# Attention's values stationary on half the array's columns, two heads side by side, and every second copy of the probabilities on VectorE

## The reference

```python
s = jnp.einsum('bhrnqd,bhrnkd->bhrnqk', qb, kb, ...) * scale
s = jnp.where(mask, s, jnp.finfo(jnp.float32).min)
m = jnp.max(s, axis=-1, keepdims=True)
p = jnp.exp(s - m)
denom = jnp.sum(p, axis=-1, keepdims=True)
o = jnp.einsum('bhrnqk,bhrnkd->bhrnqd', p, vb.astype(jnp.float32)) / denom
```

```python
outs.append(o); lses.append(lse)        # for (128,1), (512,4), (2048,16)
...
wts = jax.nn.softmax(jnp.stack(lses, axis=0), axis=0)
o = jnp.sum(wts[..., None] * jnp.stack(outs, axis=0), axis=0)
```

## Time and profile before

| | |
|---|---|
| median of 3 runs | 2057.57 us (2053.98 to 2057.8) |
| the profiled execution | 2056.82 us, span 2054.8 us |
| mean granted clock of PE, of full speed | 0.991 |
| PE busy | 1998.7 us (97%) |
| DVE, ACT, POOL busy | 1328.2, 844.9, 941.9 us |
| attention stage, first score matmul to first `q_out` | 1147.41 to 1304.64 us |

### The profile page before, as it was taken

One profiled execution on the slowest core, in us unless ns is written; L12 is line 12 of the kernel. 1 busy time (PEld: TensorE's weight loads), 2 busy tenths in 40 slices (PEclk: granted clock), 3 DMA queues, 4 the chain that ended last, 5 costly groups with the idle time before them and its releaser, 6 DMA issues.

```text
span 2054.8 us, 27393 instructions
## 1 busy us (share of the span) xinstructions
PE 1998.7 (97%) x10021; PEld 1658.6 (81%) x10021; DVE 1328.2 (65%) x1753; ACT 844.9 (41%) x1344; POOL 941.9 (46%) x548
## 2 busy tenths in 40 slices
PE   7999999999999999999999899998999999999997
PEld 6888888888887778878888689876888888888886
DVE  7887777756537654786231544698865565566977
ACT  5444454345411024562200676657333323334453
POOL 1354464333333468843453200665755555444553
PEclk8999999999999999999999999999999999999998
DMA  9223212211112243132110200132333233257344
GB/s 282 73 83 113 79 64 102 92 31 31 52 52 57 67 173 125 62 138 99 51 51 0 83 1 1 61 104 73 118 122 107 86 113 107 92 182 248 102 136 162
DMA packets 179500, 193.97 MB, mean 94 GB/s; under 512 B 9863, under 2 KB 122968, under 8 KB 179418
## 3 DMA queue, kind: packets, MB, share of 16 engines
q1 hardware_dynamic: 172996, 178.53, 27.3%
q10 hardware_dynamic: 6422, 14.37, 1.9%
HBM read 151.71 MB, written 41.16 MB: 94 GB/s over the span
## 4 chain that ended last, share of the span: by engine, by line
PE 81%; DVE 10%; ACT 4%; issue 3%; POOL 1%; DMA 0%; DVEq 0%; SPq 0%; ACTq 0%; POOLq 0%
PE psum L999 7%; PE psum L1538 7%; PE psum L1539 6%; PE psum L1540 6%; PE psum L1001 6%; PE psum L1000 6%; PE psum L1160 3%; PE psum L1641 3%; PE psum L1643 3%; PE psum L1642 3%; PE psum L1441 3%; PE psum L1020 3%; PE psum L1021 3%; PE psum L1019 3%; PE psum L1430 2%
## 5 line engine op out<-in xcount | busy, mean ns | idle before, releaser
L792 POOL TENSOR_TENSOR w_hi<-w_raw,ones 128x1024 fp32r<-128x1024 f32 x60 | 149.3, 2489 | 480.3 <-PE psum L1001 356.1
L999 PE MATMUL psum<-h_hi,w_hi 128*128 128x512 f32 x704 | 284.2, 404 | 0.0
L1001 PE MATMUL psum<-h_hi,w_lo 128*128 128x512 f32 x704 | 274.7, 390 | 0.0
L1000 PE MATMUL psum<-h_lo,w_hi 128*128 128x512 f32 x704 | 274.2, 389 | 0.0
L1673 ACT ACTIVATE arena<-psum 128x1024 f32<-128x1024 f32 (+7 forms) x134 | 100.1, 753 | 220.5 <-PE psum L1001 136.1
L795 POOL TENSOR_TENSOR w_lo<-w_raw,w_hi 128x1024 fp32r<-128x1024 f32 x60 | 168.0, 2800 | 4.7
L1000 PEld LDWEIGHTS psum<-h_lo,w_hi 128*128 128x128 f32 x704 | 132.4, 188 | 28.3 <-issue 2.6
L999 PEld LDWEIGHTS psum<-h_hi,w_hi 128*128 128x128 f32 x704 | 132.3, 188 | 28.4 <-issue 2.6
L1001 PEld LDWEIGHTS psum<-h_hi,w_lo 128*128 128x128 f32 x704 | 132.1, 188 | 28.5
L1641 PE MATMUL psum<-w_hi,h_hi 128*128 128x512 f32 x308 | 121.2, 394 | 3.1 <-DVE h_lo L3257 3.1
L989 POOL TENSOR_TENSOR w_lo<-arena,w_hi 128x512 fp32r<-128x512 f32 x61 | 86.1, 1415 | 75.7 <-ACT w_hi L1673 75.7
(11 more groups left out here) (485 smaller groups left out, 5289.0 us busy)
## 6 DMA issues: line engine op xcount, KB each, us to landing
w_raw<-w_in SPq DMA_DIRECT2D x64, 512.0 KB, 3.8
act_op<-arena SPq DMA_DIRECT2D x77, 256.0 KB, 2.3
arena<-act_op SPq DMA_DIRECT2D x77, 256.0 KB, 2.7
w_raw<-w_gate SPq DMA_DIRECT2D x22, 512.0 KB, 4.0
w_raw<-w_up SPq DMA_DIRECT2D x22, 512.0 KB, 5.2
arena<-ada_w SPq DMA_DIRECT2D x16, 512.0 KB, 7.2
arena<-w_out SPq DMA_DIRECT2D x16, 512.0 KB, 5.9
out_T<-arena SPq DMA_DIRECT2D x16, 512.0 KB, 5.6
```

The lines of the kernel that those rows point to most:

```text
L999: pe.matmul(o, wh, xh, start=(k == 0), stop=False)
L1000: pe.matmul(o, wh, xl, start=False, stop=False)
L1001: return pe.matmul(o, wl, xh, start=False, stop=(k == KT - 1))
```

## The change

1. `pv(m)` now does a pair of heads. The values (128 keys by 64 channels) are stationary, on the lower half of the array's columns for the even head and on the upper half for the odd one, and the transposed probabilities are moving, 128 columns. The result is channels by queries: even head on PSUM partitions 0 to 63, odd head on 64 to 127.
2. Since it is transposed, it must be turned back: for every four heads VectorE copies 128x256 to SBUF (`o_move`), PE transposes two 128x128 blocks (`back`), and VectorE divides from there in one instruction of 256 columns in place of two of 128 (`attended`).
3. `pt_copy` of odd steps is on VectorE, of even steps on ScalarE, with three buffers `probs_t` in place of two.
4. PE's round becomes `qk_pair(m)`, `p_t(2m-2)`, in even rounds `back`, `pv(m-2)`, `p_t(2m-1)`. The squares of `att_o` rows come three steps later on ScalarE, and at the end VectorE does `o_move(15)` ahead of the first `q_lo`.

```diff
-        probs_t = [page(22 + i) for i in range(2)]
+        probs_t = [page(i) for i in (22, 20, 23)]
+        o_t = page(26)[:, 128:384]
...
-            def pv(n):
-                i, h = n // AH, n % AH
-                pe.wait_ge(pt_done, n + 1)
-                if n >= AH:
-                    pe.wait_ge(ao_done, (n - AH) // 4 + 1)
+            def pv(m):
+                i, p = m // (AH // 2), m % (AH // 2)
+                pe.wait_ge(pt_done, 2 * m + 2)
+                if p % 2 == 0 and m >= 4:
+                    pe.wait_ge(ao_done, m // 2 - 1)
                 for j in range(i + 1):
-                    mm = pe.matmul(two_banks(3)[:, h * P:(h + 1) * P], blocks128(probs_t[n % 2], j),
-                                   v_b[:, j, (h // 2) * P:(h // 2 + 1) * P], start=(j == 0), stop=(j == i))
+                    for e in range(2):
+                        mm = pe.matmul(psum[DH * e:DH * e + DH, 6 + p // 2, (p % 2) * P:(p % 2 + 1) * P],
+                                       v_b[:, j, (2 * p + e) * DH:(2 * p + e + 1) * DH],
+                                       blocks128(probs_t[(2 * m + e) % 3], j), start=(j == 0), stop=(j == i))
                 mm.then_inc(pv_full, 1)
+            def back(g):
+                pe.wait_ge(ot_moved, OT_MOVED + g + 1)
+                for q in range(2):
+                    mm = pe.transpose(psum[:, 6 + g % 2, (2 + q) * P:(3 + q) * P], blocks128(o_t, q), ident[:])
+                mm.then_inc(ot_full, 1)
...
+            def o_move(g):
+                dve.wait_ge(pv_full, 2 * g + 2)
+                if g:
+                    dve.wait_ge(ot_full, OT_FULL + g)
+                dve.tensor_copy(o_t, psum[:, 6 + g % 2, 0:2 * P]).then_inc(ot_moved, 1)
...
+            def pt_copy(n):
+                w = (n // AH + 1) * P
+                dve.wait_ge(pt_full, n + 1)
+                if n >= 3:
+                    dve.wait_ge(pv_full, (n - 3) // 2 + 1)
+                dve.tensor_copy(probs_t[n % 3][:, 0:w], two_banks(2)[:, 0:w]).then_inc(pt_done, 1)
...
-                if n >= 6 and n % 4 == 2:
-                    attended((n - 6) // 4)
+                if n >= 7 and n % 4 == 3:
+                    o_move((n - 7) // 4)
+                if n >= 9 and n % 4 == 1:
+                    attended((n - 9) // 4)
+                if n >= 3 and n % 2:
+                    pt_copy(n - 2)
...
             q_raw_copy(5)
+            attended(2 * NT - 2)
             q_raw_copy(7)
+            o_move(2 * NT - 1)
             q_lo(0, "P1", 0)
+            q_lo(1, "P1", 1)
             attended(2 * NT - 1)
-            for j in range(1, 3):
-                q_lo(j, "P1", j)
+            q_lo(2, "P1", 2)
```

More of the change, by code:

```diff
@@ L190 @@
 N_SGU, N_SGU_SQ, N_SGU_NORM = 8, 17, 28
+OT_MOVED, OT_FULL = 5, 2
 T_ORDER = [4, 5, 6, 7, 0, 1, 2, 3]
@@ L474, in program @@
             sem("pv_full"), sem("den_done"), sem("ao_done"))
+        ot_moved, ot_full = lb_step, silu_done
         out_sent, mixn_done = sem("out_sent"), sem("mixn_done")
@@ L895, in q_sum @@
                 elif name == "S3":
+                    pool.wait_ge(pv_full, AH * NT // 2 - 1)
                     pool.wait_ge(*raw_ready(4 + j))
@@ L1459, in _ @@
             N = AH * NT
-            for m in range(N // 2 + 2):
+            for m in range(N // 2 + 1):
                 if m < N // 2:
                     qk_pair(m)
[L1463 to L1479, removed]
+                else:
+                    pe.wait_ge(mixn_done, NT)
+                    pe.wait_ge(s_moved, N)
+                    q_transpose(4)
+                    q_transpose(5)
+                if 0 <= 2 * m - N_SGU < SGU_G:
+                    sgu(2 * m - N_SGU)
+                if m >= 1:
+                    p_t(2 * m - 2)
+                if m >= 4 and m % 2 == 0:
+                    back(m // 2 - 2)
+                if m >= 2:
+                    pv(m - 2)
+                if 0 <= 2 * m + 1 - N_SGU < SGU_G:
+                    sgu(2 * m + 1 - N_SGU)
+                if m == N // 2:
+                    pe.wait_ge(*raw_ready(4))
+                    q_transpose(6)
+                    pe.wait_ge(*raw_ready(5))
+                    q_transpose(7)
+                if m >= 1:
+                    p_t(2 * m - 1)
+            pv(N // 2 - 1)
             def q_out(n, j, t):
@@ L1519, in _ @@
                     mm.then_inc(o_step, 1)
+                if n == 0:
+                    back(2 * NT - 1)
             for t in range(4):
@@ L2060, in pt_copy @@
                 act.wait_ge(pt_full, n + 1)
-                if n >= 2:
-                    act.wait_ge(pv_full, n - 1)
-                copy(probs_t[n % 2][:, 0:w], two_banks(2)[:, 0:w]).then_inc(pt_done, 1)
+                if n >= 3:
+                    act.wait_ge(pv_full, (n - 3) // 2 + 1)
+                copy(probs_t[n % 3][:, 0:w], two_banks(2)[:, 0:w]).then_inc(pt_done, 1)
             def mix_square(x, i, t, col_):
@@ L2098, in _ @@
             for n in range(N + 2):
-                if n >= 2:
+                if n >= 2 and (n % 2 == 0 or n == N + 1):
                     pt_copy(n - 2)
@@ L2115, in _ @@
                     root(M_SGU)
-                if n >= N_SGU_NORM and n % 8 == 4 and (n - 12) // 8 < NT - 1:
-                    for t in range(0 if n == N_SGU_NORM else (n - 12) // 8, (n - 12) // 8 + 1):
+                if n >= N_SGU_NORM and n % 8 == 7 and (n - 15) // 8 < NT - 1:
+                    for t in range(0 if n == N_SGU_NORM + 3 else (n - 15) // 8, (n - 15) // 8 + 1):
                         act.wait_ge(ao_done, 2 * t + 2)
@@ L2984, in _ @@
             dve.wait_ge(bias_in, 16)
+            def o_move(g):
[3 more added lines that the diff above has]
+                dve.tensor_copy(o_t, psum[:, 6 + g % 2, 0:2 * P]).then_inc(ot_moved, 1)
             def attended(m):
                 i, hh = m // 2, m % 2
-                dve.wait_ge(pv_full, 4 * m + 4)
                 dve.reciprocal(r_den[:, 4 * hh:4 * hh + 4], den_[:, 4 * m:4 * m + 4]).then_inc(den_done, 1)
                 dve.wait_ge(den_done, m + 1)
[L2992 to L2998, removed]
+                dve.wait_ge(ot_full, OT_FULL + m + 1)
+                o = att_o[:, i, hh * 256:(hh + 1) * 256].rearrange("p (h d) -> p h d", d=DH)
+                src = psum[:, 6 + hh, 2 * P:].rearrange("p (h d) -> p h d", d=DH)
+                r = r_den[:, 4 * hh:4 * hh + 4].rearrange("p (h x) -> p h x", x=1).to_broadcast([P, 4, DH])
+                TT(o, src, r, ALU.mult).then_inc(ao_done, 1)
             def q_raw_copy(k):
```

1 line of the change is left out of this document (added).

## The result

The changed kernel takes 2030.51 us (median of 4 runs, 2029.22 to 2032.28) beside 2057.22 us (4 runs, 2053.98 to 2057.8) of the kernel before, measured together: ratio 0.9876 [0.9865, 0.9888], 26.7 us less. The forecast had the sign and the mechanism, but 15.7 us less, and a range that ended at 2036.

What follows compares the result with a forecast made beforehand. PE was taken to bound five to seven blocks, ScalarE three and four. 9.3 + 4.3 + 1.5 + 3.8 - 3.2 = 15.7 us less gave 2041.1 us profiled, 2041.9 as median; range 2036 to 2055.

Steps and rivals of the forecast that it cites:

- three and four blocks: Attention rounds at three and four key blocks: ScalarE bounds them and loses eight copies, 4.3 us less.
- the cost of a block: Products of a head pair per key block in `pv`: 0.25 us in place of 0.446, bounds 0.223 and 0.27.
- the end: Behind the last `q_transpose`: first output step 2.3 us later, 0.9 us more up to step 4, together 3.2 us more.
- five to seven: Attention rounds at five to seven key blocks, bound by PE: 14.1 less 4.8, so 9.3 us less.
- eight: Eight key blocks up to the last `q_transpose`: 15.4 us of products become 11.6, 3.8 us less.
- Rival 1: Column halves do not run side by side in `pv`: 0.446 us a block, sum +13.1, 2070.7 us; chance 0.13.
- rival 2: Loads in `pv` stand in line, two of four not hidden: 0.358 us a block, about 2057 us; chance 0.13.
- The mode changes: PE entering and leaving half-column mode around each group of products: together 0.29 us.
- Rival 3: On PE's rounds, mode changes cost double (0.6 us) or VectorE's copies come late: 2046 to 2050 us; chance 0.18.
- One and two blocks: Attention rounds at one and two key blocks: three rounds by 0.5, 1.5 us less, bounds 0 and 3.
- VectorE's copies are covered: Odd steps' copies at eight blocks: 1.284 us and 0.15 for signals beside 1.60 us of scores, 0.17 to spare.
- The chain to step 4: Output steps 0 to 4: `attended(15)` waits for `back(15)`, delaying squares, root and rest, 0.9 us more.

Runs made afterwards that it cites:

- back_inside: Changed kernel with the two full transposes of `back` moved into the middle of the products of `pv`, one mode change more there and back: 2036.67 us, ratio 0.9911.
- squares_early: Changed kernel with ScalarE's squares of attention's rows back where they were (n % 8 == 4): 2036.33 us, ratio 0.9903.
- squares_late: Kernel before with only ScalarE's squares of attention's rows moved three steps later: 2054.64 us, ratio 0.9994.
- copies_split: Kernel before with only the odd steps' copies of transposed probabilities moved to VectorE, still two buffers: 2053.22 us, ratio 0.9989.
- both_on_before: Kernel before with both the later squares and the odd copies on VectorE, products on the full array: 2054.13 us, ratio 0.9989.
- in_turn: Changed kernel with the two loops of `pv` exchanged, all products of the even head ahead of the odd head's: 2048.68 us, ratio 0.9966.
- copies_act: Changed kernel with all copies of the transposed probabilities on ScalarE again: 2041.43 us, ratio 0.9922.
- rest_first: Changed kernel with VectorE's first `q_lo` put ahead of `o_move(15)`: 2031.2 us, ratio 0.9883.
- same_half: Changed kernel with both heads' products on the lower half of the columns, without accumulation over key blocks: 2060.18 us, ratio 1.0023.

## Why the prediction was wrong in its size

The mechanism was right and the sum too small. The step that failed is the one on three and four blocks; the cost of a block and the end were sized wrongly as well. By its own steps:

- **The cost of a block.** Taken 0.25 us, bounds 0.223 and 0.27; measured 0.22, the lower bound. Over 72 blocks at five to seven that is 2.2 us more, over 38 at eight 1.1 more: 9.3 becomes 11.5 for a measured 11.24, 3.8 becomes 4.9 for 5.01. Four loads of 64 columns a block hide entirely. Rival 1 (0.446) and rival 2 (0.358) are out. The Trainium skill, "TensorE: Matmul & The Clock Gate", section "The mechanism", has a sentence by which loads overlap only with matmuls of another row group, which would have given rival 2, though the same section also lets a load into the background weight buffer go ahead of running matmuls. Here both halves use all 128 rows, and two instructions, each with a load of its own, start every 0.109 us. (The 0.243 us of a full matmul in the prediction holds a pause of 0.57 us at 1312.69; the starts stand 0.227 us apart, and the argument stays as it was.)
- **The mode changes.** 0.29 a pair taken; `back_inside` gave 0.25 and 0.31. Right. Rival 3's double price is out.
- **Three and four blocks: the step that failed.** The prediction said that ScalarE "loses four copies of 0.484 and four of 0.596 us", 4.3 us, and stopped there. It overlooked that the diff takes the three squares, 3 x 0.81 = 2.4 us of ScalarE, out of this stretch too, and that PE's 27.26 us held 1.2 us of a lowered clock. ScalarE came to 21.50 in place of 24.1 us busy and PE to 22.31 in place of 25.0: 28 blocks at 0.22 and 8 rounds at 0.38 make 3.3 less, from 26.1 at full clock 22.8. PE is then the bound, and the stretch took 23.25, not 26.5. `squares_early` shows 1.87 of the 3.3 us as the squares', with the clock at 1.00 in both kernels. The 1.2 of the clock are read from PE's busy time in `squares_late`, `copies_split` and `both_on_before`; together they make 3.1 of 3.3.
- **One and two blocks.** 1.5 forecast, 1.34 measured, with bounds 0 and 3. No experiment took this apart, and executions of kernels that are the same up to there differ by up to 0.8 us in it (25.41 and 26.25 for before and `squares_late`).
- **VectorE's copies are covered.** No wait of PE for L3041 is among the waits; the copy of 1024 columns takes 1.23 us beside 1.58 us of scores. Right.
- **The end.** `pv(31)` started at T + 2.15 (forecast 2.1), PE waited 1.11 us for ScalarE ahead of it (forecast 1). Its products were through at T + 4.1, not 4.6, by the cheaper blocks. The first rest took 0.84 us (1278.97 to 1279.80), not 1.43, so step 0 came at T + 5.60, not 6.7; as the last section shows, a rest's length goes with an instruction of POOL beside it. The chain to step 4, put at 0.9 without a working, cost nothing: `attended(15)` was through 2.8 us later against step 0, but behind it stands one rest, of 0.71 us (1283.74), where before there were two, of together 3.47 us (L3010 at 1305.54). They end 4.4 us behind step 0 in both kernels. The diff moves the second `q_lo` ahead of `attended(15)`, which the prediction did not reckon with. The place and the order of the waits up to step 0 were right, the size 1.9 us too large.

In sum the forecast missed 8.2 us of the stage: 3.3 at three and four blocks, 3.2 by the cost of a block, 1.9 at the end, less 0.2 at one and two. The three large ones went the same way, and the range, which let only the block's price, the early rounds and the end vary, did not reach there. No one of them alone bridges the 5.5 us between the range's end at 2036 and the measured 2030.51. The medians missed by 11.0 us; the 2.8 beyond the 8.2 are not explained, and are of the size by which single executions differ.

## What to carry to other kernels

Where an operand is only half the array wide, two independent products on the two halves of the columns cost one, if they alternate in the program. That is shown here for fp32, 128 rows, 64 columns a half and 128 moving columns. A pair of such products saved 0.22 us, so a group is worth its change of mode (0.27 us there and back) from two pairs on. When an edit speeds the bound of one stretch, list every instruction that the diff moves out of the neighbouring engine's stretch, the small ones at its edge too, and ask of each busy time at which granted clock it was read. An edit that is worth 0.15% by itself was worth 0.5% beside one that sped up another engine, so undo edits on the changed kernel as well as adding them to the old one.

## What the runs showed of the hardware that I had not expected

**PE works ahead into the other half.** With the heads in turn, `in_turn`, some six starts around the border of the heads stand 0.05 us apart and not 0.109. How far this goes with a longer queue, or on what it depends, was not tried.

**Standing can be paid twice.** `copies_act` shows it most plainly. PE stands 2.07 us up to 1284.12, and the products behind take 3.63 us for the 1.97 of the changed kernel. Windows around that place, PEclk as the share of the full clock:

```profile
1282.00:1284.00 2.00, 0.06 (x1) 0.00 (x0) 0.57 (x1) 2.00 (x4) 2.00 (x2) 1.00 0.47 125
1284.00:1286.00 2.00, 1.88 (x18) 1.88 (x20) 0.00 (x0) 2.00 (x5) 2.00 (x3) 0.55 0.38 141
1286.00:1287.00 1.00, 1.00 (x14) 1.00 (x12) 0.00 (x0) 1.00 (x3) 1.00 (x2) 0.50 0.00 0
```

The granted clock is at 0.50 there, the lower of its two levels (1.2 for 2.4 GHz). Four kernels have the same instructions from the last `q_transpose` to step 4 and differ in how long PE stands there ahead of step 0 (stretch less PE's busy time): 1.35 us in all in `rest_first`, 2.60 in the changed kernel, 3.21 in `squares_early`, 3.51 in `back_inside`. The first two were granted 1.00 in the output steps and took 13.26 and 13.24 us; the last two 0.88, and took 14.44 and 14.42. In `back_inside` the last wait is 2.40 us, up to 1284.56; then:

```profile
1284.00:1285.00 1.00, 0.44 (x2) 0.43 (x3) 1.00 (x2) 0.29 (x1) 1.00 (x1) 1.00 0.00 0
1286.00:1287.00 1.00, 1.00 (x4) 0.81 (x3) 0.08 (x1) 0.00 (x0) 1.00 (x1) 0.50 0.00 0
```

Standing as the cause fits these five kernels, but no run changed it alone, and its length is not the whole of it: `same_half` stood 3.23 us in that place (7.97 less 4.74 busy), the last wait 2.12, with 3.71 us of products between its two waits for 1.97, and was granted 1.00 in the output steps, which took 11.49 us.

The longer standing itself comes from the two rests on VectorE, 2.54 us in the changed kernel, 3.14 in `squares_early` and 3.44 in `back_inside` for the same instructions. So 2.1 us of `back_inside` and 1.8 of `squares_early` lie outside of the place where the edit was made.

**How long a rest takes follows POOL.** The traces show what goes with a longer rest. The first rest of the changed kernel, alone, and POOL's instruction beside it; then the same two of `back_inside`:

```profile
1277.97 1.28 POOL L914 TENSOR_TENSOR arena<-spare 128x512 f32<-128x512 f32 x1
1282.48 1.28 POOL L914 TENSOR_TENSOR arena<-spare 128x512 f32<-128x512 f32 x1
1282.55 1.75 DVE L3034 TENSOR_TENSOR q_first<-spare,q_first 128x512 fp32r<-128x512 f32 x1
```

In the changed kernel the rest starts at 1278.97, POOL's instruction ends at 1279.25 and the rest at 1279.80, 0.55 us behind it. In `back_inside` the rest starts only 0.07 us behind POOL's instruction, which ends at 1283.76, and ends at 1284.30, again 0.55 behind. It is so in 49 of the 52 rests into `q_first` of the thirteen traces (0.54 to 0.55); in the other three the distance is 1.8. Beside no work of POOL one takes 0.68 us, as at 1295.99 in the changed kernel. So the 1.43 us of the earlier trace rows, which the prediction took for a cost, fits such a wait too (it is one of the 49), and how long the first output step waits depends on where in POOL's row of instructions the last `pv` ends. No run moved POOL's instructions, so that the rest waits for POOL is argued from the times alone.
